# Two transformer blocks on one core: the heads of both self attentions dealt out between weight units, memory projections first, no other data in the weight stream

## The chip, the cores and the metric

The kernel runs on one core of one Trainium2 chip. A core has five engines that work beside each other: TensorE (PE) multiplies matrices, VectorE (DVE) and ScalarE (ACT) work elementwise, GpSimd (POOL) and SyncE (SP) here only start transfers. Each engine takes its own instructions strictly in their order and waits for the others by semaphores. The metric is the device time of one execution in microseconds (us); less is better.

## The reference

Two blocks follow each other on 256 tokens of width 2048, all in float32. With rms as the scaling of each token by the root of its mean square:

```
h  = rms(x) @ w_in          -> latents of q and kv, k_rope, dq, dk, dv
q, k, v of 8 MLA heads from rms(latents) @ w_uq, w_ukv; rotation of the rope parts
mla:  softmax(q k^T) v                                     8 heads
diff: (softmax(q1 k1^T) - lam * softmax(q2 k2^T)) v        4 heads, v 256 wide; rms over each head
x += concat(mla, diff) @ w_out
x += softmax((rms(x) @ w_xq) (rms(mem) @ w_xk)^T) (rms(mem) @ w_xv) @ w_xo      4 cross heads
x += (silu(rms(x) @ w_gate) * (rms(x) @ w_up)) @ w_down
x  = rms(x)
z  = rms(x) @ w_in_2        -> aq, ak, av, rq, rk, rv, rg   (8 heads of 128 each)
moba: causal softmax(aq ak^T) av, q and k scaled per head and rotated            8 heads
ret:  ((rq rk^T) * decay mask of the head) rv, rms over each head, * silu(rg)    8 heads
x += concat(moba, ret) @ w_o_2
x += (silu(rms(x) @ w_gate_2) * (rms(x) @ w_up_2)) @ w_down_2
x += (p @ w_ple_proj_2) * sigmoid(rms(x) @ w_ple_gate_2 + b)
```

`mem` has 256 tokens, `p` is 256 x 256.

## The kernel before

All weights come in one stream of 844 units, each 128 x 1024 floats (512 KB), in the order of their use. A unit passes four hands, in a ring of four buffers (RING): SP loads it (`raw`); ScalarE rounds it to `w_hi` (`split`, L716) as soon as TensorE has finished the unit four before it (`w_used`); VectorE takes the rest, `w_lo = raw - w_hi` (`split`, L1086), which also frees the raw buffer; TensorE multiplies (`one_block`, L385). Activations are held as a hi and a lo part too (`norm_hi`, `norm_lo`, `mix_hi`, `mix_lo`), and each product is made in three passes: hi x hi, hi x lo, lo x hi, 12 matmuls of 512 columns per unit. Eight units (NU) make one block of 512 output columns, gathered in one of the two halves of the PSUM tensor `acc`; the next block but one waits until VectorE has taken it (`block_taken`). Other work of TensorE is put between two units of a block (`mid`): turning a result by transposes (`turn`, L434), above all.

A head of an attention has three groups on TensorE and steps on the others between them: `scores` (L534, L518 for retention) into a half of `acc`; VectorE finds the maxima (`maxima`, L1316, L1321); ScalarE the exponentials (`exps`, L854); VectorE divides by the sums (`normalise`, L1333 to L1348); `transposes` on TensorE (L552) and their copy by ScalarE (`copy_transposed`, L870 to L873); `values` (L571, L579) into `po`; ScalarE and VectorE keep the result (`keep`, L882 to L890, `split_head`). For retention the scores are only multiplied by the mask (L1297, L1298). Diff and retention heads are normed afterwards, scaled (L1374, L1381, L1384), turned (`turn_diff`, `turn_ret`) and split into hi and lo (`kept_hi` L753, `kept_low` L1390) as the operand of the output projection.

`attend` on each engine walks over the heads with a pipeline: at step i the scores of head i, the transposes of head i - 2, the values of head i - 3. It is called three times: for the first self attention (`FIRST_JOBS`: 4 diff heads, then 8 MLA heads), the cross attention (4 heads), the second self attention (`SECOND_JOBS`: 8 retention heads, then 8 MoBA heads). Only the first head's scores stand inside the last projection block (`first_scores`); while `attend` runs, the weight stream stands still, but for a few units near its end. Three sets of data other than weights travel in the stream: the memory (4 units, taken during the first attention by `memory`, which splits it and sums its squares), the decay masks of retention (4), and `p` (1, used by `embedding` with four one-unit blocks around the end of the second attention). The projections of the memory (w_xk, w_xv) follow the first attention: the first in `memory_keys`, its first two units inside `attend`. The token layout of x (`x_tok`, 2 MB) is loaded near the start, and ScalarE sums its squares there (L736).

The order of all this is written out by hand three times, once per engine, in one program each for TensorE, ScalarE and VectorE; the three must agree on the same units.

## Time and profile before

| | |
|---|---|
| median of 3 runs | 2496.32 us (2496.07 to 2497.47) |
| the profiled execution | 2496.18 us |
| its span, first to last instruction | 2494.4 us |
| TensorE busy | 2444.0 us, 98% |
| VectorE busy | 1407.7 us, 56% |
| ScalarE busy | 1142.7 us, 46% |
| mean granted clock of TensorE | 0.995 |

An engine's busy time is the sum of its instructions' durations without overlap. The granted clock is the share of full speed that the throttle gave TensorE; at 0.5 of it a matmul takes twice as long, and counts as busy all the while. The first attention without the stream begins at 220.15 us and reaches its last but one head at 271.52; the second runs from 1515.70 to about 1574.

### The profile page before, as it was taken

How to read it: one execution, taken by the hardware profiler on the slowest of the kernel's cores; microseconds unless marked ns; L12 is line 12 of the kernel's file. 1: busy time of each engine (PE TensorE's matmuls, PEld its weight loads, DVE VectorE, ACT ScalarE, POOL GpSimd, SP SyncE). 2: the span in 40 equal slices, each digit the busy share in tenths (PEclk: the TensorE clock that was granted, in tenths of full speed). 3: DMA queues.
4: the chain of work that ended last, by engine and by line, in shares of the span. 5: the costliest groups of instructions: out<-in, count | busy, mean ns of one | idle time of the engine just before them, and what ended most of it. 6: DMA issues, size and time to landing. Idle time of an engine off the chain costs nothing.

```text
span 2494.4 us, 31743 instructions
## 1 busy us (share of the span) xinstructions
PE 2444.0 (98%) x11244; PEld 2034.4 (82%) x11244; DVE 1407.7 (56%) x1557; ACT 1142.7 (46%) x1518; POOL 4.1 (0%) x11
## 2 busy tenths in 40 slices
PE   8999999999999999999999997999999999999998
PEld 7888788888888888888888886888888888888887
DVE  6656755655555554555665656555555455555565
ACT  6445544644434443444554445454443444344453
POOL 0000000000000000000000000000000000000000
PEclk9999999999999999999999999999999999999999
DMA  7553455465666555555556563556556555565554
GB/s 259 188 192 119 132 190 182 148 200 186 191 194 190 192 186 194 193 188 183 184 177 198 181 198 118 173 185 191 191 188 194 188 191 187 193 194 187 184 178 160
DMA packets 125465, 458.04 MB, mean 184 GB/s; under 512 B 13920, under 2 KB 14048, under 8 KB 124976
## 3 DMA queue, kind: packets, MB, share of 16 engines
q1 hardware_dynamic: 124496, 451.47, 56.0%
q0 software_dynamic: 720, 5.03, 0.5%
q8 instruction: 75, 1.23, 0.2%
q14 instruction: 30, 0.25, 0.0%
q10 hardware_dynamic: 144, 0.07, 0.0%
HBM read 454.41 MB, written 2.10 MB: 183 GB/s over the span
## 4 chain that ended last, share of the span: by engine, by line
PE 95%; DVE 2%; ACT 1%; DMA 1%; issue 0%; SPq 0%; DVEq 0%; ACTq 0%
PE acc L385 89%; PE pt L434 2%; PE acc L390 2%; PE acc L534 0%; DMA heads<-x_in 0%; PE po L571 0%; DMA x<-x_tok 0%; DVE w_lo L1086 0%; PE po L579 0%; PE pt L552 0%; ACT L772 0%; ACT w_hi L716 0%; DVE nmax L1316 0%; ACT heads L736 0%; DVE mix_lo L1184 0%
## 5 line engine op out<-in xcount | busy, mean ns | idle before, releaser
L1086 DVE TENSOR_TENSOR w_lo<-raw,w_hi 128x1024 fp32r<-128x1024 f32 x844 | 1029.3, 1225 | 944.6 <-ACT w_hi L716 937.7
L716 ACT ACTIVATE w_hi<-raw 128x1024 fp32r<-128x1024 f32 x844 | 893.8, 1060 | 1221.5 <-PE acc L385 1182.9
L385 PE MATMUL acc<-w_hi,norm_hi 128*128 128x512 f32 (+1 forms) x2320 | 907.5, 391 | 6.6 <-ACT w_hi L716 2.9
L385 PE MATMUL acc<-w_hi,norm_lo 128*128 128x512 f32 (+1 forms) x2320 | 902.6, 389 | 0.0
L385 PE MATMUL acc<-w_lo,norm_hi 128*128 128x512 f32 (+1 forms) x2320 | 618.1, 388 | 0.3 <-DVE w_lo L1086 0.3
L385 PEld LDWEIGHTS acc<-w_hi,norm_hi 128*128 128x128 f32 x2320 | 437.2, 188 | 96.4 <-ACT w_hi L716 6.6
L385 PEld LDWEIGHTS acc<-w_hi,norm_lo 128*128 128x128 f32 x2320 | 437.2, 188 | 88.4
L385 PEld LDWEIGHTS acc<-w_lo,norm_hi 128*128 128x128 f32 x2320 | 435.2, 188 | 90.2 <-DVE w_lo L1086 0.6
L385 PE MATMUL acc<-w_hi,mix_hi 128*128 128x512 f32 x1008 | 394.6, 391 | 2.3 <-DVE mix_lo L1184 2.0
L385 PE MATMUL acc<-w_hi,mix_lo 128*128 128x512 f32 x1008 | 392.4, 389 | 0.0
L385 PE MATMUL acc<-w_lo,mix_hi 128*128 128x512 f32 x1008 | 269.5, 389 | 0.0
L385 PEld LDWEIGHTS acc<-w_hi,mix_hi 128*128 128x128 f32 x1008 | 189.3, 188 | 42.0 <-issue 3.5
L385 PEld LDWEIGHTS acc<-w_lo,mix_hi 128*128 128x128 f32 x1008 | 189.2, 188 | 39.3
L385 PEld LDWEIGHTS acc<-w_hi,mix_lo 128*128 128x128 f32 x1008 | 189.4, 188 | 38.6
L1134 DVE SCALAR_TENSOR_TENSOR tmp_a<-acc,r_tok,tmp_d 128x512 f32<-128x512 f32 x44 | 31.0, 747 | 39.8 <-ACT tmp_d L791 39.8
L1128 DVE TENSOR_TENSOR x<-x,acc 128x1024 f32<-128x1024 f32 x36 | 44.0, 1221 | 12.3 <-PE acc L385 12.3
L791 ACT ACTIVATE tmp_d<-acc,r_tok 128x512 f32<-128x512 f32 x48 | 30.4, 686 | 34.9 <-PE acc L385 34.9
L534 PE MATMUL acc<-heads 128*128 128x256 f32 (+1 forms) x144 | 35.1, 384 | 7.4 <-ACT tmp_a L854 2.3
L534 PEld LDWEIGHTS acc<-heads 128*128 128x128 f32 x144 | 25.9, 198 | 12.3 <-ACT tmp_a L854 3.3
L1134 DVE SCALAR_TENSOR_TENSOR tmp_b<-acc,r_tok,tmp_a 128x512 f32<-128x512 f32 x44 | 31.0, 747 | 8.5 <-PE acc L385 8.5
L1191 DVE SCALAR_TENSOR_TENSOR norm_lo<-pt,vec,norm_hi 128x256 fp32r<-128x256 f32 x80 | 33.1, 477 | 0.4
L728 ACT ACTIVATE norm_hi<-pt,vec 128x256 fp32r<-128x256 f32 x80 | 31.1, 470 | 0.0
(196 smaller groups left out, 854.7 us busy)
## 6 DMA issues: line engine op xcount, KB each, us to landing
raw<-stream SPq DMA_DIRECT2D x853, 512.0 KB, 3.4
heads<-x_in SPq DMA_DIRECT2D x4, 512.0 KB, 10.3
x<-x_tok POOLq DMA_DIRECT2D x1, 2048.0 KB, 10.3
heads<-rows_in POOLq DMA_DIRECT2D x2, 1024.0 KB, 5.2
out<-x SPq DMA_DIRECT2D x4, 512.0 KB, 4.0
tab<-tables POOLq DMA_DIRECT2D x1, 512.0 KB, 7.2
con<-consts POOLq DMA_DIRECT2D x1, 176.0 KB, 6.2
gain_rows<-head_rows POOLq DMA_DIRECT2D x1, 128.0 KB, 7.1
```

What stands on the lines that cost most here:

```text
L385: last = pe.matmul(acc[:, slot, c * NB:c * NB + width], a[:, k * T + c * P:k * T + (c + 1) * P], w[:, s, kk * width:(kk + 1) * width], sta ...
L390: last = pe.matmul(acc[:, slot, c * T:(c + 1) * T], w[:, s, kk * NB + c * P:kk * NB + (c + 1) * P], a[:, k * T:(k + 1) * T], start=clear a ...
L434: last = pe.transpose(pt[:, c // 2, c % 2 * T + t * P:c % 2 * T + (t + 1) * P], src(c, t), ident)
L534: last = pe.matmul(acc[:, slot, at:at + width], heads[:, q * T + t * P:q * T + (t + 1) * P], heads[:, k * T:k * T + width], start=t == 0 a ...
L716: act.activation(w_hi[:, (units.fixed - 1) % RING, :], src, ACT.Copy).then_inc(w_hi_ready, 1)
L728: last = act.activation(dst[:, bass.ds(b * BCOLS + c * T, T)], src[:, c * T:(c + 1) * T], ACT.Copy, scale=gain(name, b * CB + c))
L791: last = act.activation(tile_of(tmp_d, t), tile_of(src, t), ACT.Sigmoid, scale=r_col[:, t:t + 1])
L1086: dve.tensor_tensor(w_lo[:, s, :], src, w_hi[:, s, :].bitcast(F32), ALU.subtract)\
L1128: took(dve.tensor_tensor(x_of(b), x_of(b), by_tile(src), ALU.add))
L1134: last = dve.scalar_tensor_tensor(out=tile_of(dst, t), in0=tile_of(src, t), scalar=r_col[:, t:t + 1], in1=tile_of(other, t), op0=ALU.mult, ...
L1191: last = dve.scalar_tensor_tensor(out=dst_lo[:, at], in0=src[:, c * T:(c + 1) * T], scalar=gain(name, b * CB + c), in1=dst_hi[:, at].bitca ...
```

## The change

- Every head of both self attentions is dealt out between units of the projection blocks: scores, transposes and values of a head stand some one to three units apart, and ScalarE's and VectorE's steps stand between their splits of those units (`whole` on TensorE, `during` on the other two: a table from the number of the unit in the block to what follows it). `attend` remains for the cross attention alone. MLA heads come before diff heads, MoBA before retention; the columns of w_in_2 stand in their natural order (rv before rg).
- A table `SCORED` says which block's slot of `acc` a head's scores use: the slot of the block after the one in which they stand. A block that needs the slot waits until the last scores in it have been read. The probabilities of the self attentions share tmp_d (diff: tmp_b and tmp_d) in place of three buffers.
- The projections of the memory (16 units) are the first in the stream. The memory's squares are summed by ScalarE from a token layout (`mem_squares`) in place of VectorE's products and TensorE's `memory_sums`; the keys are turned raw, and scaled later (`scale_keys`, `scale_memory`).
- The stream holds weights only. Memory comes by the SP queue at the start; x, the token layouts of x (twice, once more behind the memory's) and of the memory, the masks and `p` by the POOL queue.
- The four one-unit embedding blocks stand just ahead of the last projection (w_ple_gate_2) in place of the end of the second attention.
- The operand of the output projections for the last heads is made in the first blocks of w_out and w_o_2 (`residual(..., first=...)`).
- L numbers move: L385 becomes L422, L434 L478, L534 L572, L552 L589, L571 L610, L579 L618, L716 L746, L1086 L1122, L1316 L1345, L854 L890, L1374 L1398, L1390 L1414, L1114 L1157.

```diff
-FIRST_JOBS = [("diff", h) for h in range(DIFF_H)] + [("mla", h) for h in range(MLA_H)]
+FIRST_JOBS = [("mla", h) for h in range(MLA_H)] + [("diff", h) for h in range(DIFF_H)]
...
-SECOND_JOBS = [("ret", h) for h in range(R_H)] + [("moba", h) for h in range(A_H)]
+SECOND_JOBS = [("moba", h) for h in range(A_H)] + [("ret", h) for h in range(R_H)]
...
+SHORT = 7
+B_DQ, B_AQ = 4 + SHORT + 1, 4 + SHORT + 6 + NBD + 1 + NBD + 2 * sum(GROUPS) + NBD * len(GROUPS) + 1
+SCORED = {n: B_DQ + n // 2 for n in range(MLA_H)}
+SCORED.update({MLA_H + h: B_DQ + 4 + h // 2 for h in range(DIFF_H)})
+SCORED.update({N_MOBA + h: B_AQ + 6 + h // 2 for h in range(A_H)})
+SCORED.update({N_RET + h: B_AQ + 11 + h // 3 for h in range(R_H)})
...
+            pool.wait_ge(mem_landed[NBD - 1], 16)
+            for b in range(NBD):
+                pool.dma_start(block_of(heads, X_IN // CB + b), block_of(x_in, b)).then_inc(x_landed[b], 16)
...
             pool.dma_start(x[:, :], x_tok).then_inc(x_tok_landed, 16)
...
+            half = KC // 2 * T
+            for part in range(2):
+                pool.wait_ge(squares_ready, NBD + part * (2 + NBD // 2))
+                pool.dma_start(x[:, half:], mem_tok[:, part * half:(part + 1) * half]).then_inc(mem_tok_landed, 16)
+            pool.wait_ge(trans_done, MLA_H)
+            pool.dma_start(x[:, :], x_tok).then_inc(x_tok_landed, 16)
...
+            for half in range(2):
+                pool.wait_ge(scores_done, N_MOBA + 4 * (half + 1))
+                for i, first in enumerate((AQ, AK)):
+                    pool.dma_start(chunks(heads, first + half * CB), block_of(decay_in, 2 * i + half))                        .then_inc(decay_landed[half], 16)
...
+                last_scored = [n for n in SCORED if SCORED[n] == blocks.fixed - 1]
+                if last_scored:
+                    scores_read(last_scored[-1])
...
+                if n in SCORED:
+                    assert SCORED[n] == blocks.fixed
+                    pe.wait_ge(block_taken, blocks.fixed - 1)
+                    pe.wait_ge(heads_ready, evicts.fixed)
+                before = n - (1 if kind in WIDE else 2)
+                if before >= 0:
+                    scores_read(before)
...
-            for b in range(4):
-                one_block(NU, norm, token_major=True, mid={TURN_AT: turn_rotated})
-            one_block(NU, norm, token_major=True, mid={TURN_AT: turn_rotated})
-            one_block(NU, norm, token_major=True, mid=first_scores, mid_at=3)
...
-                          part=part)
-            last_step = len(FIRST_JOBS) + 2
-            attend(len(FIRST_JOBS), None, {last_step - 2: lambda: memory_keys(range(0, 1)),
-                                           last_step - 1: lambda: memory_keys(range(1, 2))}, started=True)
-            memory_keys(range(2, NU), {3: lambda: turn_diff(0), 4: memory_sums, 5: lambda: turn_diff(1)})
...
+            def whole(mid, act=norm):
+                one_block(NU, act, token_major=True, mid=mid)
+            whole({1: turn_rotated, 3: lambda: scores(0), 5: lambda: scores(1), 6: lambda: transposes(0),
+                   7: lambda: values(0)})
+            whole({0: lambda: transposes(1), 1: lambda: (turn_rotated(), values(1)), 2: lambda: scores(2),
+                   4: lambda: scores(3), 5: lambda: transposes(2), 6: lambda: values(2), 7: lambda: transposes(3)})
+            whole({0: lambda: values(3), 1: turn_rotated, 2: lambda: scores(4), 4: lambda: scores(5),
+                   5: lambda: transposes(4), 6: lambda: values(4), 7: lambda: transposes(5)})
+            whole({0: lambda: values(5), 1: turn_rotated, 2: lambda: scores(6), 3: turn_keys, 4: lambda: scores(7),
+                   5: lambda: transposes(6), 6: lambda: values(6), 7: lambda: transposes(7)})
+            whole({0: lambda: values(7), 1: lambda: (turn_rotated(), scores(8)), 4: lambda: scores(9),
+                   5: lambda: transposes(8)})
+            whole({0: lambda: transposes(9), 1: lambda: (values(8), scores(10)), 2: lambda: values(9),
...
             pe.wait_ge(head_split, MLA_H)
-            need = operand_need(operands.fixed)
...
+            base = operands.fixed
+            residual(NU, mix, first={0: lambda: (transposes(11), values(10)), 1: lambda: values(11),
+                                     3: lambda: turn_diff(1)},
...
+            n = N_RET
+            whole({0: lambda: values(n - 1), 1: turn_rotated})
+            whole({1: lambda: scores(n), 3: lambda: (values(n), scores(n + 1)), 5: lambda: (values(n + 1), scores(n + 2)),
+                   7: lambda: values(n + 2)})
+            whole({1: lambda: scores(n + 3), 3: lambda: (values(n + 3), scores(n + 4)),
+                   5: lambda: (values(n + 4), scores(n + 5)), 7: lambda: values(n + 5)})
+            whole({1: lambda: scores(n + 6), 3: lambda: (values(n + 6), scores(n + 7)), 4: lambda: turn_ret(0),
+                   5: lambda: values(n + 7)})
...
+            operands.add()
             for b in range(NBD):
-                one_block(NU, norm, token_major=True, need=need, mid=None if b else turn_x(NBD - 1), mid_at=TURN_AT)
+                one_block(1, mix, token_major=True, need=lambda ki: (operand_ready, base + NBD),
+                          mid={0: lambda: turn(lambda c, t: x_of(NBD - 1)[:, t, c * P:(c + 1) * P],
+                                               (block_taken, last))} if b == 1 else None)
...
-                start_hi(b)
+                mem_hi(b)
                 split(1)
-            act.wait_ge(x_tok_landed, 16)
-            for b in range(NBD):
-                token_squares(x_of(b), 0, b, block_of(heads, QN // CB + b))
-                if b % 2:
-                    split(1)
             wait_rows()
             act.activation(lam[:, 2:4], lam[:, 2:4], ACT.Exp).then_inc(func_ready, 1)
...
+            split(5)
+            for b in range(NBD):
+                x_hi(b)
+                split(1)
+            split(3)
+            for b in range(NBD):
+                x_squares(b)
+                split(1)
+            split(1)
             column_root(r_col)
...
-            attend(len(FIRST_JOBS), {
-                7: lambda: (column_root(r_head[:, :]), memory(0)),
-                9: lambda: memory(1), 11: lambda: memory(2), 12: lambda: memory(3)},
-                   started=True)
-            split(4)
-            kept_hi(8, "g_diff_sub", (0, 1, 0, 1))
-            split(2)
-            kept_hi(12, "g_diff_sub", (0, 1, 0, 1))
-            column_root(r_mem)
-            split(2)
-            split(2)
...
+            during(NU, {0: lambda: keep(7), 1: lambda: evicted(DK + CB), 2: lambda: exps(8),
+                        5: lambda: (exps(9), copy_transposed(8))})
+            during(NU, {0: lambda: copy_transposed(9), 1: lambda: keep(8), 2: lambda: (keep(9), exps(10)),
+                        4: lambda: column_root(r_head[:, 0, 0:4]), 5: lambda: (exps(11), copy_transposed(10)),
+                        6: lambda: kept_hi(8, "g_diff_sub", (0, 1, 0, 1))})
+            residual(NU, "g_xattn", {0: lambda: (copy_transposed(11), keep(10)), 1: lambda: keep(11),
+                                     2: lambda: column_root(r_head[:, 1, 0:4]),
+                                     3: lambda: kept_hi(12, "g_diff_sub", (0, 1, 0, 1))})
...
+            during(NU, {0: lambda: split_head(7), 1: lambda: maxima(8), 3: lambda: normalise(8), 4: lambda: maxima(9),
+                        6: lambda: (normalise(9), take_token_major(NU, DV, 8 * P, 0, r_col))})
+            during(NU, {1: lambda: maxima(10), 3: lambda: (head_mean(2 * P, EPS_DIFF, DIFF_H // 2, 0, 4), normalise(10)),
+                        4: lambda: maxima(11), 5: lambda: diff_scale(0),
+                        6: lambda: (normalise(11), take_token_major(NU, DV, 8 * P, 1, r_col)),
+                        7: lambda: kept_low(8, "g_diff_sub", (0, 1, 0, 1))})
+            dve.wait_ge(x_tok_landed, 2 * 16)
+            residual(NU, "g_xattn", {2: lambda: (head_mean(2 * P, EPS_DIFF, DIFF_H, 1, 4), diff_scale(1)),
+                                     3: lambda: kept_low(12, "g_diff_sub", (0, 1, 0, 1))})
...
+            n = N_RET
+            during(NU, {0: lambda: split_head(n - 1), 6: lambda: take_token_major(NU, RV, 8 * P, 0, r_col)})
+            during(NU, {1: lambda: maxima(n), 3: lambda: maxima(n + 1), 5: lambda: maxima(n + 2),
+                        6: lambda: take_token_major(NU, RV, 8 * P, 1, r_col)})
+            during(NU, {1: lambda: maxima(n + 3), 3: lambda: maxima(n + 4),
+                        4: lambda: head_mean(P, EPS, DIFF_H + R_H // 2, 0),
+                        5: lambda: (maxima(n + 5), column_inverse(r_head[:, 0, :])),
+                        6: lambda: gate(chunks(heads, RG))})
+            during(NU, {0: lambda: ret_scale(0), 1: lambda: maxima(n + 6), 3: lambda: maxima(n + 7),
+                        5: lambda: kept_low(8, "g_ret_2", range(4)),
+                        6: lambda: (head_mean(P, EPS, DIFF_H + R_H, 1), gate(chunks(heads, RG + CB))),
+                        7: lambda: column_inverse(r_head[:, 1, :])})
+            residual(NU, "g_ffn_2", {0: lambda: ret_scale(1), 3: lambda: kept_low(12, "g_ret_2", range(4, 8))})
```

What this does to the order of the instructions, at two places. First VectorE where the first output projection begins. Before the change, its steps from the last MLA heads' low halves (L1184) on: w_lo is a split of a unit, L1390 the low half of four diff chunks.

```order
L1184 TENSOR_TENSOR mix_lo<-po,mix_hi 128x256 x2
L1086 TENSOR_TENSOR w_lo<-raw,w_hi 128x1024 x4
L1390 SCALAR_TENSOR_TENSOR mix_lo<-pt,vec,mix_hi 128x256 x4
L1086 TENSOR_TENSOR w_lo<-raw,w_hi 128x1024
L1552 TENSOR_SCALAR r_tok<-po 128x2
L1086 TENSOR_TENSOR w_lo<-raw,w_hi 128x1024
L1390 SCALAR_TENSOR_TENSOR mix_lo<-pt,vec,mix_hi 128x256 x4
L1086 TENSOR_TENSOR w_lo<-raw,w_hi 128x1024
```

After the change, VectorE around the splits of units 89 to 91 (unit 88 is the first of w_out; L1203, L1395 and L1398 are root's inverse and scale of the first two diff heads, L1360 to L1369 the normalise of head 11, L1157 the eviction of half of dv, L1414 the low half of heads 8 and 9):

```order
L1203 RECIPROCAL r_head<-r_head 128x4
L1395 TENSOR_SCALAR r_head<-r_head 128x4
L1398 TENSOR_TENSOR heads<-heads,r_head 128x1024
L1122 TENSOR_TENSOR w_lo<-raw,w_hi 128x1024
L1360 RECIPROCAL row_stats<-row_stats 128x4
L1363 TENSOR_SCALAR row_stats<-row_stats,lam 128x2
L1366 TENSOR_SCALAR tmp_d<-tmp_d,row_stats 128x256 x2
L1369 SCALAR_TENSOR_TENSOR tmp_d<-tmp_d,row_stats 128x256 x2
L1157 TENSOR_SCALAR heads<-acc,r_tok 128x512 x2
L1122 TENSOR_TENSOR w_lo<-raw,w_hi 128x1024
L1414 SCALAR_TENSOR_TENSOR mix_lo<-pt,vec,mix_hi 128x256 x4
```

The low half of the first two diff heads stood behind four plain splits; now it stands behind the scale, the last head's normalise and an eviction, with a single split between each.

Second TensorE where the first attention begins. Before, from the last matmuls of the last projection block on (L534 scores, L552 transposes, L571 values):

```order
L385 MATMUL acc<-w_lo,norm_hi 128x512 x4
L534 MATMUL acc<-heads 128x256 x8
L552 MATMUL pt<-con,tmp_a 128x128 x4
L534 MATMUL acc<-heads 128x256 x4
L552 MATMUL pt<-con,tmp_b 128x128 x4
L571 MATMUL po<-heads,tmp_c 128x256 x4
L534 MATMUL acc<-heads 128x256 x4
L552 MATMUL pt<-con,tmp_d 128x128 x4
```

After, at the first scores of a diff head (L478 turns rotated keys, L572 the scores), inside a block:

```order
L422 MATMUL acc<-w_hi,norm_lo 128x512
L422 MATMUL acc<-w_lo,norm_hi 128x512 x4
L478 MATMUL pt<-con,tmp_a 128x128 x8
L572 MATMUL acc<-heads 128x256 x4
L422 MATMUL acc<-w_hi,norm_hi 128x512
L422 MATMUL acc<-w_hi,norm_lo 128x512
```

The groups of the heads stood behind each other; now a group or two stand between the twelve matmuls of one unit and those of the next.

## Rows read from the trace of the kernel before

**Rows 1.** The page: busy time by engine, and its rows of w_lo and w_hi.
```profile
PE 2444.0 (98%) x11244; PEld 2034.4 (82%) x11244; DVE 1407.7 (56%) x1557; ACT 1142.7 (46%) x1518; POOL 4.1 (0%) x11
...
L1086 DVE TENSOR_TENSOR w_lo<-raw,w_hi 128x1024 fp32r<-128x1024 f32 x844 | 1029.3, 1225 | 944.6 <-ACT w_hi L716 937.7
...
L716 ACT ACTIVATE w_hi<-raw 128x1024 fp32r<-128x1024 f32 x844 | 893.8, 1060 | 1221.5 <-PE acc L385 1182.9
```

**Rows 2.** Stretches: span, busy us (instructions) by engine, granted clock, DMA share, GB/s.
```profile
28.14:54.22 26.08, 22.82 (x130) 20.62 (x129) 17.61 (x36) 20.91 (x39) 0.00 (x0) 0.93 0.55 181
30.79:35.24 4.45, 4.45 (x13) 3.50 (x14) 2.44 (x6) 4.43 (x11) 0.00 (x0) 0.62 0.34 118
220.15:271.52 51.37, 42.52 (x201) 35.52 (x201) 39.97 (x96) 36.78 (x113) 0.00 (x0) 0.93 0.14 45
265.02:270.15 5.13, 5.13 (x15) 4.25 (x16) 4.26 (x9) 4.66 (x13) 0.00 (x0) 0.51 0.23 89
1515.70:1574.03 58.33, 43.04 (x222) 34.49 (x221) 39.85 (x110) 32.47 (x112) 0.53 (x1) 0.91 0.27 92
1540.62:1545.80 5.18, 5.18 (x18) 4.11 (x18) 2.89 (x12) 3.29 (x10) 0.00 (x0) 0.50 0.00 0
```

**Rows 3.** TensorE by line, 220.15 to 271.52: count, busy us, mean ns, idle before.
```profile
L534 PE MATMUL acc<-heads 128*128 128x256 f32 x88 | 20.9, 383 | 3.8 <-DVE heads L1114 1.5 <-ACT tmp_b L854 1.3 <-ACT tmp_d L854 0.9
L571 PE MATMUL po<-heads,tmp_c 128*128 128x256 f32 x32 | 7.6, 379 | 0.0
L579 PE MATMUL po<-tmp_c,heads 128*128 128x256 f32 x24 | 7.1, 422 | 0.0
```

**Rows 4.** TensorE's timeline, first stage: start, busy us, count, idle before.
```profile
231.57 1.89 PE L534 MATMUL acc<-heads 128*128 128x256 f32 x8
233.30 0.60 PE L552 MATMUL pt<-con,tmp_d 128*128 128x128 f32 x4
233.73 1.89 PE L571 MATMUL po<-heads,tmp_c 128*128 128x256 f32 x8
...
265.02 1.12 PE L552 MATMUL pt<-con,tmp_b 128*128 128x128 f32 x4 [4.30 <-DVE tmp_b L1348]
```

**Rows 5.** TensorE's timeline, second stage.
```profile
1524.22 0.82 PE L518 MATMUL acc<-heads 128*128 128x256 f32 x4
...
1525.54 0.82 PE L518 MATMUL acc<-heads 128*128 128x256 f32 x4
...
1540.62 0.87 PE L552 MATMUL pt<-con,tmp_a 128*128 128x128 f32 x3 [4.40 <-DVE mix_lo L1390]
```

**Rows 6.** TensorE's timeline: scores between two units of the stream.
```profile
207.53 1.89 PE L534 MATMUL acc<-heads 128*128 128x256 f32 x8
```

**Rows 7.** ScalarE and VectorE by line and shape, whole span: busy us, mean ns.
```profile
L1114 DVE TENSOR_SCALAR heads<-acc,r_tok 128x512 f32<-128x512 f32 x14 | 9.9, 747 | 2.1 <-PE acc L385 2.1
...
L854 ACT ACTIVATE tmp_a<-acc,nmax 128x256 f32<-128x256 f32 x15 | 6.9, 471 | 1.8 <-DVE nmax L1321 1.8
...
L1390 DVE SCALAR_TENSOR_TENSOR mix_lo<-pt,vec,mix_hi 128x256 fp32r<-128x256 f32 x16 | 6.6, 477 | 2.3 <-ACT mix_hi L753 2.3
...
L882 ACT ACTIVATE heads<-po 128x512 f32<-128x512 f32 x4 | 2.4, 600 | 0.5 <-PE po L571 0.5
...
L1374 DVE TENSOR_TENSOR heads<-heads,r_head 128x1024 f32<-128x1024 f32 x2 | 2.4, 1218 | 0.0
```

**Rows 8.** VectorE's timeline, normalise and next maxima of a diff head.
```profile
227.28 0.18 DVE L1333 RECIPROCAL rowsum<-rowsum 128x4 f32<-128x4 f32 x1 [0.28 <-ACT tmp_b L854]
...
229.33 1.23 DVE L1316 TENSOR_REDUCE nmax<-acc 128x4 f32<-128x1024 f32 x1
```

**Rows 9.** ScalarE's timeline at a switch of its function table.
```profile
247.48 1.28 ACT L772 ACT_TABLE_LOAD   x1
248.77 0.21 ACT L772 ACTIVATE r_head<-r_head 128x8 f32<-128x8 f32 x1
```

**Rows 10.** TensorE's timeline at a one-unit block of the embedding.
```profile
1567.30 0.47 PE L385 MATMUL acc<-w_hi,norm_hi 128*128 128x512 f32 x1 [0.44 <-issue]
```

738 lines of the change are left out of this document (341 added, 397 removed).

## The prediction

> **What bounds the kernel now.** I read the page first, then the kernel by stretches, TensorE's timeline where the stretches lose time, and last the other two engines there. The page says that TensorE works for 98% of the span, so the most that a reordering can give is what TensorE loses, not what VectorE or ScalarE are busy [rows 1]. A weight unit needs 1.06 us of ScalarE and 1.225 us of VectorE [rows 1]; TensorE gives it 12 matmuls at .227 us each, 2.72 us. In the stream TensorE therefore sets the pace, and the 944.6 us of idle time before VectorE's w_lo are waits for a weight buffer.
>
> The stretches show three places where TensorE's time is lost [rows 2]:
> - Start. Between 28.14 and 54.22 us TensorE is busy for 22.82 of 26.08 us. Most of the idle 3.26 us is one gap: ScalarE takes the token squares of x before the next unit's w_hi. Behind it 4.45 us run at a granted clock of 0.62, which costs 4.45 x .38 = 1.7 us.
> - First attention stage, 220.15 to 271.52: 51.4 us. Its work at full clock is counted from the groups [rows 3] and from pitches in TensorE's timeline, from start to start [rows 4]: eight matmuls of 256 columns take 233.30 - 231.57 = 1.73 us, one head's transposes .43. So 88/8 x 1.73 = 19.0 for scores, (32 + 24)/8 x 1.73 = 12.1 for values, 11 x .43 = 4.7 for transposes, 2.7 for the unit inside: 38.5 us. Lost: 12.9. The two largest pieces stand in rows: a wait of 4.30 for the probabilities at 265.02 [rows 4], and the clock of 0.51 behind it, 5.13 x .49 = 2.5 us [rows 2]. VectorE and ScalarE were preparing the memory just there.
> - Second attention stage, 1515.70 to 1574.03: 58.3 us. A pair of scores and values of a retention head takes 1525.54 - 1524.22 = 1.32 us [rows 5]. With 16 such pairs less one scores group (21.1 - .65), 8 groups of transposes (3.4), one turn of eight transposes (.9) and four units (10.9) the work is 35.7 us. Lost: 22.6, with 4.40 of it in one wait at 1540.62 [rows 5] and the clock of 0.50 behind that [rows 2].
> The rest of the span is the stream itself, which the change does not shorten: 844 units before and after.
>
> **The start, term by term.** The memory projections come first, then the projection of x; the squares of x move behind unit 25, with one unit's split between two of them. The gap of 3.26 us becomes a wait of about .4 (the Sin switch stands before a w_hi; bounds 0 and 2.65), and the half clock behind it goes: -2.9 - 1.7 = -4.6. The POOL queue now carries x_in, x_tok twice, the token copy of memory and the decays. The stream's queue loses nine loads of half a megabyte, so the traffic through the first 30 us stays about what it was; I cost it at nothing, hidden behind a stream that keeps three units ahead. Without that cover the price would be a late raw buffer, bounded by one such gap, 2.65.
>
> **The first stage.** -12.9 goes, and .4 for the memory sums' matmuls: -13.3. What TensorE does for a head stays the same; it now stands between units. An isolated group costs hardly more than a group in a row: the scores at 207.53 began as soon as the stream let them [rows 6]. I take .04 us per place, 1.2 for 34 places. Then the new waits. VectorE and ScalarE work strictly in order, three to four units ahead of TensorE; whatever needs the newest unit's result makes everything behind it late.
> a) Scores of head 8 stand right behind the turn of rotated keys and need that turn's eviction. In the kernel before the same kind of eviction (L1114) held up the stage's first scores, by 1.5 [rows 3]. I take 1.5; bounds 0 and 1.5.
> b) The turn of diff heads 8 and 9 before unit 87 needs the scale, which VectorE reaches only after maxima, normalise and two w_lo. From the end of the values of head 9: keep 1.3 (a copy of .60 and two squares), four exponentials 1.9 [rows 7], w_hi 1.06, w_lo 1.225, mean .17, normalise 229.33 - 227.28 = 2.05 [rows 8], w_lo 1.225, maxima 1.22 + .17, w_lo 1.225, inverse and scale .4 + 1.22 [rows 7], with four hand-overs of .25: 14.1 us. TensorE has 13.1 us of work in between. Wait 1.0; bounds 0 and 2.
> c) The first unit of w_out, 88, needs the low half of heads 8 and 9 (kept_low). VectorE does that after w_lo(91), for which it needs w_hi(91), and that needs the buffer of unit 87. But w_lo(91) stands in turn behind the normalise of head 11 (2.05) and the two-part eviction of the diff values (2 x .747, with overlap 1.4 [rows 7]), and these behind w_lo(90). From the end of unit 87: ScalarE, late by a table switch, the exponentials of head 11 and the kept_hi of heads 8 and 9, ends kept_hi as unit 87 ends. VectorE runs w_lo(90) until -.4, normalise until 1.65, eviction until 3.1, w_lo(91) until 4.3, then kept_low 4 x .477 = 1.65 with overlap [rows 7]: 5.95. I take 5.9. If ScalarE and the normalise are through in time, the lower bound is .25 + 1.06 + 1.225 + 1.65 + .25 + hand-overs = 4.7; the upper bound is 7, with one more w_lo. This is the largest new cost. It is like the 4.30 and the 4.40 of before in length, so the clock behind it should fall as it did there: 2.4 [rows 2].
> d) The second turn of diff heads, before unit 92, needs the scale that stands behind w_lo(94). From the end of unit 90: w_hi(94) 1.06, table 1.28 [rows 9], root, inverse and scale 1.8, hand-overs .6: 4.7, and TensorE has one unit of 2.72. Wait 2.0; bounds 1 and 3. Some lowered clock behind a, b and d: .8, between nothing and one more 2.5.
> In the blocks with MLA heads I find no wait: a value group is ready about .4 us before it is due. Sum: 1.2 + 1.5 + 1.0 + 5.9 + 2.4 + 2.0 + .8 = 14.8; with -13.3 the first stage comes out at +1.5.
>
> **The second stage.** -22.6 goes. Back come 1.2 for 35 places, 1.2 for the turn of the second four retention heads (the same chain as in d, less its margin of one more unit; bounds 0 and 3), and 1.2 for the one-unit blocks of the embedding. Those four blocks of one unit are still one-unit blocks, before each of which TensorE now idles for .44 us for "issue" [rows 10]. Maxima of MoBA heads and the retention products have two units each, and the normalised rotation of queries was already in the stream. Net -19.0. The final row scaling, the residual blocks and the MLPs keep their order but for the embedding's low half beside the last turn, .7 us of VectorE inside a unit where it has 1.5 us free: nothing.
>
> **The sum.** -4.6 + 1.5 - 19.0 = -22.1. The profiled execution has a span of 2494.4 and took 2496.18, 1.8 more than its span; the median of the runs is 2496.32. 2494.4 - 22.1 = 2472.3, and + 1.8 gives 2474.1: 2474 us.
>
> **Rivals.**
> R1, all new waits are hidden: VectorE is only 56% busy, and each wait of a to d is a difference of two sums near each other, c excepted. Then -4.6 - 13.3 - 22.6 + 1.2 + 1.2 + 1.2 = -36.9, so 2459. Against it: c is a chain of three weight-buffer steps that no free time shortens.
> R2, the dealt heads are later than I find: copy to values in MLA blocks has .4 us of slack, and with a drift of .35 to .7 us at some 18 of the 69 places comes 9, with one more half-clock stretch 11: 2485. For it: the scores of the first stage waited 1.3 and .9 for exponentials even where nothing else ran [rows 3]; here a w_hi of 1.06 stands between as well. Against: each head has more units beside it than before.
> R3, slower. Each place where a group enters the stream costs the .44 us "issue" gap that stands before the units at 1567.30 and behind [rows 10]: 69 x .44 = 30, on top of the 2474: 2504. It decides from .32 us a place on (22.1/69), where the gain is gone. Against it: the scores of 207.53 and turns inside the stream show no such gap, and what 1567.30 has special is the start of a new block of one unit. The change has 69 places of the kind of 207.53 [rows 6].
> R4, table switches cost more than their row. ScalarE's switch of functions took 1.28 us, and the next ACTIVATE began .01 us behind it [rows 9]. If the stretch before it hid as much again, b, c and d would each be 1.3 longer: 2478. The Trainium skill, "ScalarE: Activation LUTs", section "What ACT_TABLE_LOAD costs", has such a rule: about 1283 ns for the load and a drain of about 1380 ns beside it at every switch. The load of this trace agrees with it (1.28); behind the load this trace shows no drain, and before it I find none in these two rows.
>
> **How the numbers follow.** Forecast 58%, with its own range 2466 to 2481 (c, d and the lowered clock at their bounds). R1 12%, R2 19%, R3 6%, R4 5%. A range of 2462 to 2488 holds the forecast's case, R2, R4 and a third of R1; it leaves out R3, most of R1 and a tail of R2. A measurement of this kernel tells .2%, 5 us, from no change. Faster by more than that: all but R3 and R2's tail, .91; within it .03; slower .06.
>
> **What would show it.** In the profile of the changed kernel: no gap of 2.5 us and no lowered clock between 28 and 54 us (start). One wait of 4.7 to 7 us before the first unit of w_out for kept_low's mix_lo, with a clock near 0.5 behind it (c), and 1 to 2 us before the turn of diff heads twice (b, d). Waits under .5 us behind scores, transposes and values everywhere between units 40 and 86 and in the second input projection (no R2). TensorE's busy time down by the lowered clock of the two stages only, its idle time by some 15 us. Wrong would be: an "issue" gap at the inserted groups (R3), waits for a raw buffer in the first 60 us (the POOL queue's loads), or no wait at w_out (R1).

## The result, and the profile after

The changed kernel takes 2469.6 us (median of 4, 2469.07 to 2469.99) against 2496.34: a ratio of 0.9892, 95% interval 0.9875 to 0.9909. That is 26.7 us less where 22 were forecast (2474), inside the range. Its profiled span is 2468.2, against 2494.4: 26.2 less, and that is the number taken apart below.

The page after, the lines that answer to [rows 1]:

```profile
PE 2434.5 (99%) x11240; PEld 2029.3 (82%) x11240; DVE 1398.0 (57%) x1554; ACT 1146.3 (46%) x1537; POOL 10.4 (0%) x23
...
L1122 DVE TENSOR_TENSOR w_lo<-raw,w_hi 128x1024 fp32r<-128x1024 f32 x844 | 1029.5, 1225 | 943.3 <-ACT w_hi L746 936.2
...
L746 ACT ACTIVATE w_hi<-raw 128x1024 fp32r<-128x1024 f32 x844 | 894.2, 1061 | 1234.8 <-PE acc L422 1191.4
```

The work per unit is the same. TensorE's idle time fell from 50.4 us (2494.4 - 2444.0) to 33.7, its busy time by 9.5, though it does the same matmuls but for the memory sums. Most of the second is lowered clock that went: some 6 us by the clocks of the slow stretches, [rows 2] and the one named below. The rest of it is not accounted for. By stretches, as in [rows 2]:

```profile
22.00:60.00 38.00, 37.89 (x168) 31.06 (x167) 30.40 (x49) 26.56 (x47) 0.53 (x1) 1.00 0.85 307
...
118.00:326.00 208.00, 198.66 (x925) 165.24 (x924) 121.49 (x180) 106.66 (x197) 1.59 (x3) 0.98 0.47 158
...
304.02:309.20 5.18, 5.18 (x15) 4.08 (x16) 0.00 (x0) 0.02 (x1) 0.00 (x0) 0.57 0.22 83
...
1380.00:1560.00 180.00, 179.04 (x859) 149.78 (x858) 107.45 (x148) 86.92 (x151) 2.11 (x4) 1.00 0.56 181
```

Between 22 and 60 us TensorE idles for .1 us where it idled for 3.3, at full clock. The dealt first attention, 118 to 326 us, still idles for 9.3 us and has one stretch at 0.57, 5.18 us long. The dealt second one, 1380 to 1560, idles for 1.0 us in 180: the 4.40 us wait [rows 5] and both slow stretches are gone, the one of [rows 2] at 1540.62 and one ahead of it (0.62 over 1518.50 to 1523.00). Where TensorE waits after, over the whole execution (engine, tile and line that waited, then what for, us in total, count, longest; the rows of the cross attention and of TensorE's very first instruction are not shown):

```profile
PE acc L422 <- DVE mix_lo L1414: 4.5, 1, 4.5
...
PE acc L422 <- DVE mix_lo L1226: 2.8, 1, 2.8
...
PE acc L422 <- DVE mix_lo L1219: 2.0, 2, 1.0
...
PE pt L478 <- ACT tmp_c L909: 1.8, 1, 1.8
...
PE pt L478 <- DVE heads L1398: 1.7, 1, 1.7
...
PE acc L572 <- issue: 1.3, 1, 1.3
...
PE pt L478 <- DVE heads L1408: 1.0, 1, 1.0
```

L1226 is the wait before the first unit, L1219 two waits in the MLPs, both as before. The others are new, and they are the forecast's four and the last retention turn. The one for "issue" is the forecast's a): the profile names nothing that released it, but ScalarE's eviction of the turn ran from 245.33 to 246.33, and the scores began at 246.43.

To sum up without reading every wait, I took from TensorE's timeline the start of each unit, and from each distance to the next start 2.72 us: what is left is everything but units, lost or not.

| us outside units | before | after | measured | forecast |
|---|---|---|---|---|
| from the first unit to 60 us | 6.9 | 2.9 | -4.1, first unit .3 later: -3.8 | -4.6 |
| from 60 us to the end of the cross attention | 81.8 | 80.9 | -.9 | +1.5 |
| from there to the end | 91.6 | 70.1 | -21.5 | -19.0 |

The three add up to -26.2.

### The profile page after: what moved, and what is told of

It reads as the page before. It is cut to its first block, busy times and chain, and to the rows that moved or that the text cites. A ratio compares the mean times of both kernels' runs of the same rounds, so it can differ in the third digit from the quotient of the medians.

```text
span 2468.2 us, 31637 instructions
## 1 busy us (share of the span) xinstructions
PE 2434.5 (99%) x11240; PEld 2029.3 (82%) x11240; DVE 1398.0 (57%) x1554; ACT 1146.3 (46%) x1537; POOL 10.4 (0%) x23
## 4 chain that ended last, share of the span: by engine, by line
PE 97%; DVE 2%; ACT 1%; DMA 1%; issue 0%; ACTq 0%; SPq 0%; DVEq 0%
PE acc L422 90%; PE pt L478 2%; PE acc L427 2%; PE acc L572 1%; PE po L618 1%; DVE w_lo L1122 1%; PE po L610 0%; PE pt L589 0%; DMA raw<-stream 0%; ACT w_hi L746 0%; DMA vec<-vectors 0%; PE acc L556 0%; ACT mix_hi L765 0%; DVE mix_lo L1226 0%; DVE mix_lo L1219 0%
## 5 line engine op out<-in xcount | busy, mean ns | idle before, releaser
L1122 DVE TENSOR_TENSOR w_lo<-raw,w_hi 128x1024 fp32r<-128x1024 f32 x844 | 1029.5, 1225 | 943.3 <-ACT w_hi L746 936.2
L746 ACT ACTIVATE w_hi<-raw 128x1024 fp32r<-128x1024 f32 x844 | 894.2, 1061 | 1234.8 <-PE acc L422 1191.4
L422 PE MATMUL acc<-w_hi,norm_hi 128*128 128x512 f32 (+1 forms) x2240 | 881.2, 394 | 0.0
L422 PE MATMUL acc<-w_hi,norm_lo 128*128 128x512 f32 (+1 forms) x2240 | 869.5, 388 | 0.0
L422 PE MATMUL acc<-w_lo,norm_hi 128*128 128x512 f32 (+1 forms) x2240 | 596.2, 388 | 0.0
L422 PEld LDWEIGHTS acc<-w_lo,norm_hi 128*128 128x128 f32 x2240 | 419.4, 188 | 86.6
L422 PEld LDWEIGHTS acc<-w_hi,norm_lo 128*128 128x128 f32 x2240 | 420.8, 188 | 84.1
L422 PEld LDWEIGHTS acc<-w_hi,norm_hi 128*128 128x128 f32 x2240 | 420.7, 188 | 83.9
L422 PE MATMUL acc<-w_hi,mix_hi 128*128 128x512 f32 x1088 | 428.6, 394 | 9.3 <-DVE mix_lo L1414 4.5
L422 PE MATMUL acc<-w_hi,mix_lo 128*128 128x512 f32 x1088 | 425.5, 391 | 0.0
L422 PE MATMUL acc<-w_lo,mix_hi 128*128 128x512 f32 x1088 | 292.0, 390 | 0.0
L422 PEld LDWEIGHTS acc<-w_hi,mix_hi 128*128 128x128 f32 x1088 | 205.4, 189 | 52.9 <-issue 7.6
L422 PEld LDWEIGHTS acc<-w_lo,mix_hi 128*128 128x128 f32 x1088 | 205.3, 189 | 43.0
L422 PEld LDWEIGHTS acc<-w_hi,mix_lo 128*128 128x128 f32 x1088 | 205.5, 189 | 41.9
L1226 DVE SCALAR_TENSOR_TENSOR norm_lo<-pt,vec,norm_hi 128x256 fp32r<-128x256 f32 x80 | 33.1, 476 | 0.5
L572 PE MATMUL acc<-heads 128*128 128x256 f32 (+1 forms) x112 | 27.8, 366 | 4.0 <-ACT tmp_a L890 1.4
L1219 DVE TENSOR_TENSOR mix_lo<-pt,mix_hi 128x1024 f32 (+1 forms) x22 | 26.8, 1218 | 0.0
```

What stands on the lines that cost most here:

```text
L422: last = pe.matmul(acc[:, slot, c * NB:c * NB + width], a[:, k * T + c * P:k * T + (c + 1) * P], w[:, s, kk * width:(kk + 1) * width], sta ...
L572: last = pe.matmul(dst[:, at:at + width], src[:, q * T + t * P:q * T + (t + 1) * P], heads[:, k * T:k * T + width], start=t == 0 and i == ...
L746: act.activation(w_hi[:, (units.fixed - 1) % RING, :], src, ACT.Copy).then_inc(w_hi_ready, 1)
L1122: dve.tensor_tensor(w_lo[:, s, :], src, w_hi[:, s, :].bitcast(F32), ALU.subtract)\
L1219: dve.tensor_tensor(dst, src, hi.bitcast(F32), ALU.subtract).then_inc(done, 1)
L1226: last = dve.scalar_tensor_tensor(out=dst_lo[:, at], in0=src[:, c * T:(c + 1) * T], scalar=gain(name, b * CB + c), in1=dst_hi[:, at].bitca ...
```

## The experiments

All but the last are the changed kernel with an edit; all ran beside the kernel before. A kernel's own runs lie .1 to 2.8 us apart from lowest to highest, and those of the kernel before, over all rounds, 6.4 (2494.29 to 2500.65): differences under 1 us (next to the kernel before, under 2) are read from the traces and not from the medians.

**e1_need: what the first unit of w_out waits for**

```diff
-                     first_need=lambda ki: (operand_ready, base + (ki * UK >= 12)))
+                     first_need=lambda ki: (operand_ready, base - 1 + (ki * UK >= 8) + (ki * UK >= 12)))
```

> The first unit of w_out waits only for the operand that it reads (the eight MLA heads), no longer for the low half of diff heads 8 and 9. Theory A (the 4.46 us wait there, the 2.85 us that the unit behind it runs longer at the lowered clock, and .3 beside them, hang on this one wait): 4.5 + 2.85 + .3 = 7.6 less, 2462 us, and no wait above .5 us at that place. Rival B (VectorE is late anyway, so the next units wait for w_lo, or the wait before the second diff turn grows by as much): 2467 to 2470 us, with a new wait of 2 to 5 us behind the place.

2465.27 us, 4.3 less, between the two. TensorE's timeline:

```profile
304.09 0.63 PE L589 MATMUL pt<-con,tmp_d 128*128 128x128 f32 x4 [1.85 <-DVE mix_lo L1414]
```

Unit 88 no longer waits, but behind it head 11's transposes wait 1.85 us for the same low half. They write the transposition buffer `pt`, which that step reads. So the low half held two things, and the narrower need freed one: 2.6 us of the wait, and 2.0 by the clock, which stays full here. (The 2.85 of the expectation was mis-read: the unit behind the wait carries values of twice the length that I had counted; e2_low_first shows its length at full clock, 4.85 us against 6.88.) The wait before the second diff turn is 1.75 as it was. Theory A holds for the clock and fails for the wait.

**e2_low_first: the order on VectorE**

```diff
-                        6: lambda: (normalise(11), take_token_major(NU, DV, 8 * P, 1, r_col)),
-                        7: lambda: kept_low(8, "g_diff_sub", (0, 1, 0, 1))})
+                        6: lambda: (kept_low(8, "g_diff_sub", (0, 1, 0, 1)), normalise(11),
+                                    take_token_major(NU, DV, 8 * P, 1, r_col))})
```

> VectorE makes the low half of heads 8 and 9 ahead of the normalise of head 11 and the eviction of the second half of dv, instead of behind them and one more w_lo. Theory A (the wait before w_out is VectorE's order: normalise 2.05, eviction 1.4, w_lo 1.23 stood ahead): the low half would end at about 300.1 of the changed kernel's trace instead of 303.9; the wait falls from 4.46 to about .8 and the clock behind it stays full: 2469.6 - 3.7 - 2.9 = 2463 us. Rival C (the wait is the weight buffer's chain w_hi(91), w_lo(91) from the end of unit 87): the wait stays near 4.4, 2469 us.

2464.15 us, 5.5 less, the wait .69. Theory A holds, rival C falls: the wait was VectorE's order.

```profile
299.77 0.47 PE L422 MATMUL acc<-w_hi,mix_hi 128*128 128x512 f32 x1 [0.69 <-DVE mix_lo L1414]
```

From the start of unit 87 to that of unit 89 it is 5.8 us less than in the changed kernel: 3.8 by the wait, 2.0 by the clock.

**e7_copy_first: what the first diff turn waits for**

```diff
-                        4: lambda: column_root(r_head[:, 0, 0:4]), 5: lambda: (exps(11), copy_transposed(10)),
+                        4: lambda: column_root(r_head[:, 0, 0:4]), 5: lambda: (copy_transposed(10), exps(11)),
```

> ScalarE copies head 10's transposes before it takes the exponentials of head 11, instead of behind them. The turn of diff heads 8 and 9 shares the transposition buffer with these transposes. Theory F (the 1.85 us wait before that turn is for the copy, which stood behind a table switch and four exponentials; behind it comes VectorE's scale, ready at about 294.7 of the changed kernel's trace, 1.0 us earlier): the wait falls to about .9 and now names VectorE's scale: 2468.7 us. Rival G (the scale was the last all along): wait 1.85, 2469.6 us.

The wait fell from 1.85 to .84 and names the scale, as theory F has it; but the time did not move (2469.66), where theory F had 2468.7:

```profile
294.04 1.09 PE L478 MATMUL pt<-con,heads 128*128 128x128 f32 x8 [0.84 <-DVE heads L1398]
...
303.33 0.76 PE L422 MATMUL acc<-w_hi,mix_hi 128*128 128x512 f32 x1 [5.44 <-DVE mix_lo L1414]
```

The next wait, before w_out, grew from 4.46 to 5.44; the two together are 6.3 us in both kernels. VectorE's normalise there stands behind w_lo(90), and ScalarE gives it w_hi(90) only behind both the copy and the exponentials of head 11, in whichever order: at the same time as before. A wait ahead of a longer wait for another chain is free, and so is taking it away. I had priced it by itself; that was wrong.

**e5_squares: the start**

```diff
             for b in range(NBD):
                 x_squares(b)
-                split(1)
-            split(1)
+            split(5)
             column_root(r_col)
```

> The four groups of token squares of x, some 4.9 us of ScalarE, stand behind each other, without a unit's w_hi between them. Theory H (the gap of 2.65 us near 28 us of the kernel before came from waiting for x_tok in that place, and ScalarE's lead of three units, 3 x 2.72 - 1.06 = 7.1 us, hides 4.9 us of work): no new wait, 2469.6 us within .7. Rival I (the bulk of the squares ahead of a w_hi made the gap): a wait of 2 to 3 us and the lowered clock behind it, 2472 to 2474 us.

2469.33 us. Theory H holds: even undivided, from 52.59 us on, the squares hide behind ScalarE's lead. TensorE has one wait between 12 and 120 us, and it ends 24 us before the squares begin. TensorE, then ScalarE:

```profile
28.30 0.50 PE L422 MATMUL acc<-w_hi,mix_hi 128*128 128x512 f32 x1 [0.72 <-ACT w_hi L746]
```

```profile
26.78 0.53 ACT L978 ACTIVATE tmp_c<-tmp_c 128x384 f32<-128x384 f32 x1 [1.94 <-DVE tmp_c L1457]
...
52.59 0.61 ACT L773 ACTIVATE heads<-x 128x512 f32<-128x512 f32 x1
```

That wait is for a w_hi behind the Sin (L978), which the edit does not touch. The first unit began at 9.16 us in this execution and at 9.91 in that of the changed kernel, and the same w_hi ends the lead of both: the later start has the shorter wait. Up to 60 us both spend the same outside units, 3.0 and 2.9 us.

The kernel before lost its 2.65 us behind a wait of ScalarE for x_tok in that place (its rows by line give 5.7 us of idle time before the squares of x, all for that transfer). The squares' work alone makes no gap, as this run shows; by the timeline the transfer alone would hardly have made one either, for without the four squares between, w_hi would have begun at 27.23 in place of 29.69 and ended at about 28.3, where TensorE was ready at 28.14. No run parts the two in the kernel before.

**e6_tables: the price of a table switch**

```diff
-                                     2: lambda: column_root(r_head[:, 1, 0:4]),
+                                     2: lambda: (load_table(ACT.Sqrt, 0), load_table(ACT.Exp, 1), column_root(r_head[:, 1, 0:4])),
```

> Two more switches of ScalarE's function table, each with a one-column ACTIVATE, ahead of the root of diff heads 10 and 11, on the path to the second diff turn (wait 1.74 us now). Theory J (a switch costs its 1.28 us and nothing beside): the wait grows by 2 x 1.28 + .3 = 2.9 to 4.6 us, 2472.5 us, up to 2475 with the lowered clock behind so long a wait. Rival K (a drain of 1.38 us beside every load, as the Trainium skill, 'ScalarE: Activation LUTs', section 'What ACT_TABLE_LOAD costs', has it): the wait grows by 5.3 to 5.6, to 7.2 us, 2475 to 2478 us.

2474.99 us. ScalarE's timeline over the added switches, and TensorE's wait behind them:

```profile
318.86 1.28 ACT L940 ACT_TABLE_LOAD   x1
...
320.15 0.20 ACT L940 ACTIVATE r_head<-ones 128x1 f32<-128x1 f32 x1
...
320.36 1.28 ACT L940 ACT_TABLE_LOAD   x1
```

```profile
325.10 1.12 PE L478 MATMUL pt<-con,heads 128*128 128x128 f32 x4 [4.69 <-DVE heads L1398]
```

From one load to the next is 1.50 us: 1.28 for the load, .22 for the one-column ACTIVATE. The wait grew from 1.74 to 4.69, by 2.95: theory J. Most of the rest of the 5.4 us that the median moved is the clock, 0.51 from 325.10 to 331.00. The Trainium skill's figure of 1283 ns for the load ("ScalarE: Activation LUTs", section "What ACT_TABLE_LOAD costs") agrees; its drain of 1380 ns at each switch to a different set does not show here, neither as a gap nor in the wait.

**u1_first: the first attention in one piece**

```diff
-            whole({1: turn_rotated, 3: lambda: scores(0), 5: lambda: scores(1), 6: lambda: transposes(0),
-                   7: lambda: values(0)})
...
+            for b in range(3):
+                whole({1: turn_rotated})
+            whole({1: turn_rotated, 3: turn_keys})
+            whole({1: turn_rotated})
+            whole({})
+            pe.wait_ge(heads_ready, evicts.fixed)
+            attend(0, MLA_H + DIFF_H)
...
-            residual(NU, mix, first={0: lambda: (transposes(11), values(10)), 1: lambda: values(11),
-                                     3: lambda: turn_diff(1)},
+            residual(NU, mix, first={0: lambda: turn_diff(0), 3: lambda: turn_diff(1)},
```

ScalarE's and VectorE's tables are taken apart in the same way. The first unit of w_out waits only for what it reads, as in e1_need.

> The first self attention in one piece again, between the last projection block and w_out, with all else as in the changed kernel (memory first and out of the stream, the same order of heads, the diff turns behind units 88 and 91, the narrower need of w_out). Theory D (dealing the heads is what pays): the stage loses about 13 us as it did before, against 12.4 us of waits and lowered clock of the dealt stage: about 2470 us or more, up to 2480. Rival E (what cost time in the old stage was the memory's work on VectorE and ScalarE beside it, not that the heads stood together): waits of 1.5 at the start, 1 to 2 at each end, 2 to 3 before the first diff turn, 7 to 9 us in all: 2464 to 2467 us, faster than the changed kernel.

2464.73 us (2463.84 to 2465.66): 4.9 less than with the heads dealt out as in the change. Rival E's forecast is met. Part of the 4.9 is not the one piece: the dealt kernel with the same narrower need takes 2465.27 us (e1_need), and with one step of VectorE moved 2464.15 (e2_low_first), both level with this one within the spread of its runs. Where TensorE waits in the stage:

```profile
PE pt L477 <- DVE heads L1385: 1.9, 1, 1.9
...
PE pt L588 <- DVE tmp_b L1356: 1.6, 2, 1.2
...
PE acc L571 <- DVE heads L1144: 1.6, 1, 1.6
```

The stage as a stretch:

```profile
255.32:302.74 47.42, 43.59 (x222) 36.68 (x220) 31.65 (x85) 31.94 (x102) 1.04 (x2) 1.00 0.25 89
```

The stage takes 47.4 us for 42.5 of work (the unit at its start, 12 heads, 4 of them wide, at the pitches of [rows 4]), and 1.9 more before the first diff turn; the clock stays at 1.00. So 4.9 are lost, and 1.9 behind; the same kind of stage lost 12.9 before [rows 2], when VectorE and ScalarE split the memory and summed its squares beside its last heads. Whether that work made the difference, or the order of the heads, is what b1_no_memory asks, below.

**u2_second and u2b_second: the second attention in one piece**

u2_second does to the second attention what u1_first does to the first; u2b_second changes it further:

```diff
-            attend(N_MOBA, A_H + R_H)
+            attend(N_MOBA, A_H)
+            attend(N_RET, R_H, 1)
```

with the values of a retention head one step behind its scores in place of three.

> The second self attention in one piece again, behind the last projection block, MoBA first, all else as in the changed kernel (the masks loaded apart, the embedding at the end). Theory D: VectorE needs 2.5 us per MoBA head against TensorE's 1.75, 6 us over eight heads; start 1.5; turns of the retention heads 2.8 and 2.5; lowered clock 2.5 to 5; less the .96 of now: 14 to 17 us more, 2484 to 2487 us. Rival E (the gain of the second stage came from masks and embedding out of it): under 7 us more, below 2477 us.

2490.87 us: 21.3 more than the changed kernel, above theory D's figure. Six waits of .8 us at the retention heads, for the products behind the mask, were not in it.

> The second self attention in one piece as in u2_second (2490.9 us), but MoBA and retention as two pieces, the values of a retention head right behind the next head's scores as in the kernel before, so that the six waits of .8 us for the products behind the mask go. Theory D (even a well ordered piece loses more than the dealt heads, by waits at its start and end, VectorE's pitch per MoBA head and the lowered clock): 4.8 less for these waits, 1 to 3 more for the MoBA heads' end, 2487 to 2489 us, still 17 to 19 above the changed kernel. Rival E (the order of the retention heads made most of the loss): 2478 us or less.

2486.12 us (2484.24 to 2486.77), 16.5 more. By its profiled span, which is that of its fastest execution, it is 14.1 more, 2482.3 against 2468.2. This is far from rival E and a little below theory D's figure. TensorE's timeline in u2b_second:

```profile
1513.26 2.13 PE L570 MATMUL acc<-heads 128*128 128x128 f32 x8 [2.85 <-issue]
...
1518.02 1.65 PE L570 MATMUL acc<-heads 128*128 128x128 f32 x4 [2.63 <-ACT tmp_d L883]
...
1527.99 0.55 PE L587 MATMUL pt<-con,tmp_d 128*128 128x128 f32 x3 [0.28 <-DVE tmp_d L1365]
...
1530.23 0.55 PE L587 MATMUL pt<-con,tmp_d 128*128 128x128 f32 x3 [0.27 <-DVE tmp_d L1365]
...
1552.34 1.09 PE L476 MATMUL pt<-con,heads 128*128 128x128 f32 x8 [2.52 <-DVE heads L1401]
```

A stretch behind its first wait:

```profile
1515.00:1520.00 5.00, 2.37 (x8) 1.69 (x8) 2.84 (x13) 3.01 (x9) 0.00 (x0) 0.50 0.32 108
```

Two waits of 2.7 at the start, one of 2.5 before the turn, a clock of 0.50 behind the first two, and a pitch of 2.24 us (1530.23 - 1527.99) for a MoBA head that has 1.75 of TensorE's work: TensorE waits for VectorE there. Dealt out, the same head has whole units of 2.72 us between its groups. But 5.5 of the 14.1 us are the two waits at the piece's own start, where the kernel before, with its first scores inside the last block, waited 1.5 (at 1517.36). No run has a piece with that start and without the masks and the embedding, so u2b_second bounds what dealing is worth here from above and does not measure it.

**best: the changed kernel without its ordered waits**

e1_need, e2_low_first and e7_copy_first together, and these steps, here as TensorE, ScalarE and VectorE have them (the maxima and exponentials of head 8 stand one unit later too):

```diff
-            whole({0: lambda: values(7), 1: lambda: (turn_rotated(), scores(8)), 4: lambda: scores(9),
+            whole({0: lambda: values(7), 1: turn_rotated, 2: lambda: scores(8), 4: lambda: scores(9),
...
-                                     2: lambda: column_root(r_head[:, 1, 0:4]),
+            residual(NU, "g_xattn", {..., 1: lambda: (keep(11), column_root(r_head[:, 1, 0:4])),
...
-            residual(NU, "g_xattn", {2: lambda: (head_mean(2 * P, EPS_DIFF, DIFF_H, 1, 4), diff_scale(1)),
+            residual(NU, "g_xattn", {1: lambda: (head_mean(2 * P, EPS_DIFF, DIFF_H, 1, 4), diff_scale(1)),
...
-                        7: lambda: column_inverse(r_head[:, 1, :])})
-            residual(NU, "g_ffn_2", {0: lambda: ret_scale(1), 3: lambda: kept_low(12, "g_ret_2", range(4, 8))})
+                        7: lambda: (column_inverse(r_head[:, 1, :]), ret_scale(1))})
+            residual(NU, "g_ffn_2", {3: lambda: kept_low(12, "g_ret_2", range(4, 8))})
```

> The changed kernel with its waits of the first stage and of the last retention turn taken away by order: low half of heads 8 and 9 ahead of the normalise, the narrower need of w_out, copy of head 10 first, scores of head 8 one unit behind the turn, root and scale of heads 10 and 11 one unit earlier, scale of the last retention heads one unit earlier. Theory A (each wait hangs on one order and frees TensorE): 5.45 as measured alone for the low half, and .7 + .9 + 1.3 + 1.75 + .96 = 5.6 more: 2458.5 us. Rival B (they move to the next place): between 2461 and 2464 us.

2460.06 us (2459.91 to 2460.12; ratio to the kernel before .9852, interval .9836 to .9869): 9.5 less than the changed kernel, 1.6 above theory A and .9 below rival B's range. The waits for head 8, for the second diff turn and for the last retention turn are gone. What is left in the first stage:

```profile
255.71 1.97 PE L572 MATMUL acc<-heads 128*128 128x256 f32 x8 [0.68 <-ACT tmp_b L890]
...
294.10 1.09 PE L478 MATMUL pt<-con,heads 128*128 128x128 f32 x8 [0.84 <-DVE heads L1398]
...
301.04 0.65 PE L589 MATMUL pt<-con,tmp_d 128*128 128x128 f32 x4 [0.38 <-DVE tmp_d L1369]
...
302.45 1.97 PE L610 MATMUL po<-heads,tmp_c 128*128 128x256 f32 x8 [0.76 <-ACT tmp_c L909]
```

The .68 at 255.71 is new (the exponentials of head 8 are one unit later now, and the next wide scores need their place), as are .38 and .76 behind unit 88: together 1.8, which is what theory A missed.

**b1_no_memory: the kernel before, its work on the memory shrunk**

```diff
-                dve.tensor_tensor(mem_squares if m else mem_sums, src, src, ALU.mult).then_inc(sums_ready, 1)
+                dve.tensor_tensor((mem_squares if m else mem_sums)[:, 0:1], src[:, 0:1], src[:, 0:1], ALU.mult).then_inc(sums_ready, 1)
```

and in the same way the other operations of `memory` on both engines, and the sums behind them. The kernel leaves out the memory's split and squares but for one column of each chunk, so its cross attention is not that of the reference.

> This is the kernel before, not the changed one. Left out: ScalarE's and VectorE's work on the memory during the first attention (its split and its squares) is done for one column of each chunk, with the same instructions, waits and transfers; some 12 us of VectorE and 4 us of ScalarE go. Theory M (the first stage of the kernel before lost its time to this work beside the last heads, not to the heads standing together): the wait of 4.30 us at 265.02 and most of the lowered clock behind it (2.5) go, and parts of the waits of .95 and .72 ahead of it: 6 to 8 us less than the kernel before. Rival N (the loss is the pipeline of the heads itself, or their order): less than 2 us less.

2489.59 us (2487.87 to 2490.64; ratio to the kernel before .9968, interval .9957 to .9980): 7.8 less than the kernel before beside it (2497.42), 6.8 less than its first median, with theory M's 6 to 8 around both. By unit starts, the time outside units between 60 us and the end of the cross attention is 74.4 in place of 81.8: 7.4 less, with 1.5 more at the start, which the edit does not touch. TensorE's waits between 215 and 285 us:

```profile
PE acc L534 <- DVE heads L1118: 1.5, 1, 1.5
...
PE acc L534 <- ACT tmp_b L854: 1.3, 1, 1.3
...
PE pt L552 <- DVE tmp_b L1352: 1.1, 1, 1.1
```

And the stretch at the end of the stage, where the kernel before waited 4.30 us and then ran at a clock of 0.51:

```profile
255.00:275.00 20.00, 18.89 (x93) 15.55 (x92) 13.44 (x45) 11.83 (x37) 0.00 (x0) 1.00 0.29 92
```

Theory M holds. u1_first has 7.0 less than the kernel before in the same stretch. It differs in the order of its heads too, but the memory's work alone is large enough for all that the old stage lost against it.

## Why the prediction was right, and where its steps were off

**The start (forecast -4.6, measured -3.8): right in mechanism.** The gap and the lowered clock went, and the forecast's wait of .4 behind the Sin is there as .26: 2.98 us from 25.97 to 28.95 for a unit of 2.72. What was not forecast is the first unit: it begins .3 later and takes .3 longer (9.91 to 15.08, before 9.63 to 14.51), which is most of the .8. I named the squares' work as the cause of the gap; e5_squares shows that it makes none by itself, and the trace has ScalarE waiting 5.73 us for their transfer ahead of it.

**First stage (+1.5, measured -.9): the four waits were there, each in its place.**
a) 1.5 forecast, 1.29 measured.

b) 1.0 forecast, 1.85 measured. This step named the wrong chain. VectorE's scale did end when the forecast had it, and would have given the wait forecast. But the turn also needs the transposition buffer, and ScalarE copied head 10's transposes out of it only behind a table switch and four exponentials. VectorE's scale, then ScalarE, then TensorE, each in its own timeline:

```profile
293.45 1.23 DVE L1398 TENSOR_TENSOR heads<-heads,r_head 128x1024 f32<-128x1024 f32 x1
```

```profile
291.89 1.28 ACT L890 ACT_TABLE_LOAD   x1
...
293.18 0.48 ACT L890 ACTIVATE tmp_d<-acc,row_stats 128x256 f32<-128x256 f32 x1
...
294.99 0.61 ACT L909 ACTIVATE tmp_c<-pt 128x512 f32<-128x512 f32 x1
```

```profile
295.74 1.06 PE L478 MATMUL pt<-con,heads 128*128 128x128 f32 x8 [1.85 <-ACT tmp_c L909]
```

The scale ends at 294.7, the copy at 295.6, and the turn begins at 295.74. e7_copy_first shows that the copy was last, and that the part of the wait which it took away, 1.0 us, had cost nothing while c stood behind it.

c) 5.9 forecast, 4.46 measured, and the unit behind it, with its two groups, 2.0 longer by the clock (2.4 forecast). The order of the chain was right; it was mis-sized by its start. VectorE began the normalise 1.7 us before unit 87 ended at 299.4 (298.49, the start of its last four matmuls, and 4 x .227), not .4 before it:

```profile
297.72 0.17 DVE L1360 RECIPROCAL row_stats<-row_stats 128x4 f32<-128x4 f32 x1
...
299.64 1.40 DVE L1157 TENSOR_SCALAR heads<-acc,r_tok 128x512 f32<-128x512 f32 x2
...
301.07 1.23 DVE L1122 TENSOR_TENSOR w_lo<-raw,w_hi 128x1024 fp32r<-128x1024 f32 x1
...
302.22 1.65 DVE L1414 SCALAR_TENSOR_TENSOR mix_lo<-pt,vec,mix_hi 128x256 fp32r<-128x256 f32 x4
```

From there on the steps are the forecast's: normalise, eviction 1.4, w_lo, low half 1.65, to 303.9; the unit began at 304.02. b's longer wait had held unit 87 back by .85 us while VectorE's chain ran on, so an error in b came back in c: together they are 6.3, where the forecast had 6.9. e2_low_first is the proof of the order, and e1_need shows what the forecast did not see, that the transposes behind unit 88 hang on the same step.

d) 2.0 forecast, 1.74 measured. The .8 for further lowered clock: nothing; behind the waits of 1.3 to 1.85 us the granted clock stayed at 1.00, behind the one of 4.46 it did not. Between unit starts each of the four waits costs .2 to .3 more than its row says (4.74 at w_out), 1.1 in all, which the forecast lacked.

**Insertion (1.2 + 1.2 forecast, where .04 us at 34 and 35 places makes 1.4 each): nothing.** A group between units costs no more than in a row. Retention's groups in the stream:

```profile
1464.69 0.47 PE L422 MATMUL acc<-w_hi,norm_hi 128*128 128x512 f32 x1
...
1467.52 0.39 PE L422 MATMUL acc<-w_hi,norm_hi 128*128 128x512 f32 x1
...
1470.24 0.83 PE L610 MATMUL po<-heads,tmp_c 128*128 128x128 f32 x6
...
1470.90 0.82 PE L556 MATMUL acc<-heads 128*128 128x256 f32 x4
...
1471.48 0.48 PE L422 MATMUL acc<-w_hi,norm_hi 128*128 128x512 f32 x1
```

Values and the next scores with a unit behind them, 1467.52 to 1471.48, take 3.96 us: 2.72 + 1.24. The unit behind a group takes .11 longer (2.83, 1464.69 to 1467.52), which makes 1.35, where the pair takes 1.32 in a row [rows 5]. R3 falls: the only "issue" wait at all 69 places is a).

**Second stage (-19.0, measured -21.5).** The last turn waits .96 (1.2 forecast). The embedding's 1.2 did not come back. I had read its "issue" gap as a property of one-unit blocks [rows 10]; in the changed kernel the same four blocks have none. In the kernel before, VectorE's copy of an earlier embedding block ran from 1565.98 to 1567.20, and the unit began at 1567.30. That fits a wait for the block's half of `acc`; no run tests it apart.

Over-priced were insertion (2.4), c (1.4), the embedding (1.2), the clock (1.2), d (.3), a and the last turn (.2 each): 6.9. Against them stand b (.9), the start (.8) and the 1.1 beside the waits: 2.8. That is the 4.1 us by which the span forecast, 2472.3, was high. So part of the closeness is luck: errors of both signs met.

**The rivals.** R1 (all waits hidden) was wrong at w_out, as argued. R2 (drift in the dealt heads): no head of MLA or MoBA waits between units at all; the copy of an MLA head ends at 239.1 and its values begin at 240.47, 1.3 us of slack where I had .4. R4: refuted by e6_tables.

**What the forecast did not ask** is which part of the change pays. It booked the old stage's loss as gained by dealing, so the number says nothing on that. For the second attention dealing may be most of it: in one piece, as written here, it costs 14 to 16.5 us more. For the first it is not: the memory's work was some 7 of the 13 us, and in one piece, with the memory out of the way, it is 4.9 us faster than dealt as in the change. That is no price of dealing as such: one need or one step mended makes the two level (2465.3 and 2464.2 against 2464.7), and with its waits ordered dealing wins by some 4 us (best, without the gain of .96 at the retention turn: 2461.0), against a piece whose own 6.8 us of waits nobody ordered. What is open: what the rest of the second stage's gain (21.5 less 14 to 16.5) owes to the masks' and the embedding's new places, and what to the order of its heads; no run parts them.

## What to carry to other kernels

Before dealing a stage out between other work, find what made the stage slow: here one of two stages was slowed by foreign work on the helper engines, and some 7 of its 13 us went with that work alone. When each engine has one hand-written order, price a wait by every resource that the waiting instruction names, buffers too, and take waits away from the longest chain on: a short wait ahead of a longer one for another chain is free. Narrowing a need helps only if nothing close behind needs the same step.

## What the runs showed of the hardware

- Groups of 128- and 256-column matmuls between units of 512 columns cost TensorE nothing extra (1.35 us for a pair, with what the unit behind it takes longer, against 1.32 in a row).
- In the changed kernel and its edits the granted clock stayed at 1.00 behind waits of .7 to 1.85 us and fell to about 0.5 behind waits of 4.46 and 4.69 (0.57 and 0.51 over 5 to 6 us). The same wait of 4.46 had different prices: the unit behind it took 6.29 us in e5_squares, 6.88 in the changed kernel and 7.59 in u2_second, against 4.85 at full clock. In between the length of a wait does not decide by itself. Behind a wait of 2.52 us in u2b_second the clock stayed at 1.00, behind one of 2.54 in u2_second it fell to 0.50:

```profile
1552.34:1557.34 5.00, 5.00 (x26) 4.31 (x27) 3.55 (x7) 2.63 (x5) 0.00 (x0) 1.00 0.29 105
```

```profile
1559.50:1562.50 3.00, 3.00 (x9) 2.35 (x8) 1.42 (x4) 1.57 (x4) 0.00 (x0) 0.50 0.45 168
```

- In the kernel before it fell 2 us behind a wait of 1.50 (at 1517.36). What sets it off is open.
- A switch of ScalarE's function table took 1.28 us wherever it stood, with the next ACTIVATE .01 behind it where that waited for nothing else.
